# The output projection's weights and its first row tile are loaded during attention, and that tile is worked on in halves

## The reference

```python
o = bidirectional_retention(...)                      # 4 heads of 128
ret_out = silu(rg) * groupnorm(o) * ret_gn_w          # columns 0:512
mla_out = rms_norm(mla_attention(...), mla_out_norm_w)  # 8 heads of 64, columns 512:1024
mix = concatenate([ret_out, mla_out], axis=-1) @ w_out
x = layer_norm(DN_ALPHA * x + mix, ln1_w, ln1_b)
affinity = softmax(x @ w_router)                      # then: each of 16 experts picks its top tokens
```

## Time and profile before

| what | value |
|---|---|
| median of 3 runs | 3680.98 us (3678.96 to 3681.22) |
| profiled execution | 3676.88 us, its span 3675.1 us |
| TensorE busy | 3467.4 us, 94% of the span |
| DVE, ACT, POOL busy | 61%, 43%, 23% |
| attention's last DVE instruction starts | 1753.48 us |
| output stage's first DMA issue | 1757.43 us |
| first projecting matmul of tile 0, of tile 1 | 1770.85, 1791.43 us |
| output stage's last DVE instruction starts | 2105.14 us |

### The profile page before, as it was taken

The page is one execution under the profiler, slowest core; times in us unless marked ns, Lnnn a source line. Parts: engine busy times, 40 slices in busy tenths (PEclk is TensorE's granted clock), DMA queues, the critical chain, the costliest instruction groups (busy, mean ns, idle before and its releaser), DMA issues. The chain is left out here.

```text
span 3675.1 us, 51638 instructions
## 1 busy us (share of the span) xinstructions
PE 3467.4 (94%) x19042; PEld 2957.8 (80%) x19042; DVE 2239.5 (61%) x3925; ACT 1590.4 (43%) x2038; POOL 831.6 (23%) x412
## 2 busy tenths in 40 slices
PE   8999979997999999999799859999999999999996
PEld 6888868885777777777577649999999999999996
DVE  5444457776888888886455465555555555555568
ACT  2111134443676777767332223333333333333466
POOL 0000000003676767767011101111111111111101
PEclk9999989997999999999899869999999999999998
DMA  3111145656133332210433335555555555555676
GB/s 119 62 63 62 64 163 196 214 197 184 32 56 58 57 57 40 50 32 7 158 131 133 116 99 167 167 166 165 167 164 166 167 165 166 165 167 163 194 256 211
DMA packets 342352, 474.65 MB, mean 129 GB/s; under 512 B 105648, under 2 KB 241584, under 8 KB 339536
## 3 DMA queue, kind: packets, MB, share of 16 engines
q1 hardware_dynamic: 329344, 427.10, 37.1%
q0 software_dynamic: 12880, 45.88, 5.6%
HBM read 355.54 MB, written 117.39 MB: 129 GB/s over the span
## 5 line engine op out<-in xcount | busy, mean ns | idle before, releaser
L63 PE MATMUL psum<-xeT_hi,w_hi 128*128 128x320 f32 x2048 | 634.4, 310 | 0.0
L65 PE MATMUL psum<-xeT_hi,w_lo 128*128 128x320 f32 x2048 | 632.8, 309 | 0.0
L64 PE MATMUL psum<-xeT_lo,w_hi 128*128 128x320 f32 x2048 | 632.8, 309 | 0.0
L1357 POOL TENSOR_TENSOR added<-added,p_hi 128x1024 f32<-128x1024 f32 x192 | 458.8, 2389 | 157.4 <-ACT p_hi L1311 156.5
L2267 DVE TENSOR_TENSOR w_lo<-w_raw,w_hi 128x2048 fp32r<-128x2048 f32 x190 | 427.5, 2284 | 30.7 <-ACT w_hi L2102 30.7
L2102 ACT ACTIVATE w_hi<-w_raw 128x2048 fp32r<-128x2048 f32 x192 | 358.4, 1908 | 187.1 <-PE psum L65 187.1
L1393 DVE TENSOR_TENSOR p_lo<-psum,p_hi 128x1024 fp32r<-128x1024 f32 x272 | 332.5, 1222 | 89.4 <-ACT psum L1313 88.4
L63 PEld LDWEIGHTS psum<-xeT_hi,w_hi 128*128 128x128 f32 x2048 | 384.4, 188 | 0.9
L64 PEld LDWEIGHTS psum<-xeT_lo,w_hi 128*128 128x128 f32 x2048 | 384.4, 188 | 0.6
L65 PEld LDWEIGHTS psum<-xeT_hi,w_lo 128*128 128x128 f32 x2048 | 384.4, 188 | 0.0
L1311 ACT ACTIVATE p_hi<-psum 128x1024 fp32r<-128x1024 f32 x272 | 279.3, 1027 | 218.4 <-PE psum L65 218.3
(11 more groups left out here) (364 smaller groups left out, 7165.5 us busy)
## 6 DMA issues: line engine op xcount, KB each, us to landing
w_raw<-in_w_gate SPq DMA_DIRECT2D x64, 1024.0 KB, 5.2
w_raw<-in_w_up SPq DMA_DIRECT2D x64, 1024.0 KB, 7.4
w_raw<-in_w_down SPq DMA_DIRECT2D x64, 1024.0 KB, 5.4
rec<-rec SPq DMA_DIRECT2D x20, 768.0 KB, 3.6
recb<-rec SPq DMA_DIRECT2D x20, 768.0 KB, 5.0
xa<-in_x SPq DMA_DIRECT2D x20, 512.0 KB, 4.5
xb<-in_x SPq DMA_DIRECT2D x20, 512.0 KB, 5.8
v_lo_hi<-v SPq DMA_DIRECT2D x16, 640.0 KB, 9.6
```

What stands on the lines that cost most here:

```text
L63: pe.matmul(out, a[0], b[0], start=first, stop=False)
L64: pe.matmul(out, a[0], b[1], start=False, stop=False)
L65: return pe.matmul(out, a[1], b[0], start=False, stop=last)
L1357: g.tensor_tensor(acc[:], so_far, p_hi[at % 4][:].bitcast(F32), ALU.add).then_inc(s["p_added"], 1)
```

## The change

A buffer `c.shared`, 128 x (9 x 1024 + 8) float32, is allocated once for all stages. It takes the place of buffers that each stage had for itself: the weight staging, row tiles and some temporaries of the two retention stages, and the MoE stage's `w_raw` (4 x 2048) and `y_part`. Attention has nothing of its own in it; to make room there, its `added`, the first two of four `p_hi` and the first two of four `p_lo` move to memory of the latents, which attention did not use before. During attention SP loads into `shared` all 8 slices of `w_out` (two in each of the heads 1 to 4, at slots 22 and 24) and, at slot 20 of the last head, `feature_w` and tile 0 of `cat`, its attention half behind a wait for the stores of that half. The output stage then splits the slices from `shared`. Its tile 0 is turned, weighed and split in halves of 4 slices, the second half's work stands between the weight slices 0 and 1, tile 1's rms and scaling stand ahead of slice 4, and tile 1's turn behind the matmuls of slice 4. DVE's wait for the constants moves to the first use of `ln_w`.

```diff
@@ attention_phase
+        AHEAD_LOADS = {SLOTS * (n // 2 + 1) + 22 + 2 * (n % 2): n for n in range(DK)}
+        FIRST_CAT = SLOTS * (MH - 1) + 20
+        turn_at = [g + 2 for g in last_of]
-        added = [sb(f"added{b}", [P, 2, 512]) for b in range(2)]
+        wide = lambda at: at.rearrange("p (z n) -> p z n", z=2)
+        added = [wide(latents[4][:, D * b:D * (b + 1)]) for b in range(2)]
-        p_hi = [sb(f"p_hi{b}", [P, 2, 512], F32R) for b in range(4)]
-        p_lo = [sb(f"p_lo{b}", [P, 2, 512], F32R) for b in range(4)]
+        p_hi, p_lo = ([wide(latents[2 + a][:, D * b:D * (b + 1)]) for b in range(2)]
+                      + [sb(f"p_{n}{b}", [P, 2, 512], F32R)[:] for b in (2, 3)] for a, n in enumerate(("hi", "lo")))
@@ sync
+                    if g in AHEAD_LOADS:
+                        k = AHEAD_LOADS[g]
+                        sp.dma_start(wo_raw(c, k), d["w_out"][k * P:(k + 1) * P, :]).then_inc(ahead_in, 16)
+                    if g == FIRST_CAT:
+                        sp.dma_start(feature_weights(c), d["feature_w"]).then_inc(ahead_in, 16)
+                        sp.dma_start(first_cat(c)[:, 0:RW], d["ret"][0]).then_inc(ahead_in, 16)
+                        for b in range(2):
+                            sp.wait_ge(o_out[b], 16 * sum(1 for n in range(NBH) if n % 2 == b and turn_at[n] + 1 <= g))
+                        sp.dma_start(first_cat(c)[:, RW:D], d["o"][0].rearrange("p h e -> p (h e)")
+                                     ).then_inc(ahead_in, 16)
+                sp.wait_ge(ahead_in, 16 * (DK + 3))
@@ output_phase, sync
-                load_cat(0, 0)
-                sp.dma_start(fw[:], d["feature_w"]).then_inc(s["fw_in"], 16)
-                load_w(sp)
@@ tensor
+                def turn_first():
+                    for half, done in ((0, "turned_a"), (1, "turned")):
+                        if half == 1:
+                            pe.wait_ge(s["scaled"], 1)
+                        for k in range(4):
+                            at = 4 * half + k
+                            ins = pe.transpose(ps[:, half, k * P:(k + 1) * P], cat[0][:, at * P:(at + 1) * P], c.ident)
+                        ins.then_inc(s[done], 1)
                 def project_first():
-                    pe.wait_ge(s["lo_made"], 1)
+                    pe.wait_ge(s["lo_a_made"], 1)
                     for k in range(DK):
-                        pe.wait_ge(w_ready, k + 1)
+                        if k == 4:
+                            pe.wait_ge(s["lo_made"], 1)
+                        pe.wait_ge(s["w_lo_made"], k + 1)
...
-                    turn(1, 1)
+                        if k == 4:
+                            turn(1, 1)
-                turn(0, 0)
+                turn_first()
@@ scalar
-                scale(0, 0, 32)
-                make_hi(0, 0)
-                w_make_hi(a)
+                def w_make_hi(k):
+                    a.activation(w_hi[:, k, :], wo_raw(c, k), ACT.Copy).then_inc(s["w_hi_made"], 1)
+                scale(0, 0, 0)
+                a.wait_ge(s["weighted_a"], 1)
+                a.activation(cat_hi[0][:, 0:4, :], weighted[:, 0:4, :], ACT.Copy).then_inc(s["hi_a_made"], 1)
+                w_make_hi(0)
+                a.wait_ge(s["weighted"], 1)
+                a.activation(cat_hi[0][:, 4:DK, :], weighted[:, 4:DK, :], ACT.Copy).then_inc(s["hi_made"], 1)
+                for k in range(1, DK):
+                    if k == 4:
+                        scale(1, 1, 32)
+                    w_make_hi(k)
@@ vector
+                        if isinstance(u, int) and u == 1:
+                            v.wait_ge(s["const_in"], 48)
                         v.tensor_tensor(r[:], r[:], ln_w[:], ALU.mult).then_inc(s["ln_weighted"], 1)
-                v.wait_ge(s["fw_in"], 16)
+                def weigh_first(half, turned, weighted_done, hi_done, lo_done):
...
                 rms(0)
-                weigh(0, 0)
-                w_make_lo(v)
-                v.wait_ge(s["const_in"], 48)
+                weigh_first(0, s["turned_a"], s["weighted_a"], s["hi_a_made"], s["lo_a_made"])
+                w_make_lo(0)
+                weigh_first(1, s["turned"], s["weighted"], s["hi_made"], s["lo_made"])
+                for k in range(1, DK):
+                    if k == 4:
+                        rms(1)
+                    w_make_lo(k)
@@ moe_phase
-        raw = [sb(f"w_raw{r}", [P, CH]) for r in range(4)]
+        raw = [c.shared[:, CH * r:CH * (r + 1)] for r in range(4)]
-        y_part = sb("y_part", [CAP_S, 2, 512])
+        y_part = c.shared[0:CAP_S, 8 * D:9 * D].rearrange("p (a n) -> p a n", a=2)
```

More of the change, by code:

```diff
@@ L70, in bc, with wo_raw, first_cat, feature_weights @@
     return ap.unsqueeze(axis).to_broadcast(shape)
+def wo_raw(c, k):
+    return c.shared[:, D * k:D * (k + 1)]
+def first_cat(c):
+    return c.shared[:, DK * D:DK * D + D]
+def feature_weights(c):
+    return c.shared[:, 9 * D:9 * D + DK]
 class Core:
@@ L105, in split_weights @@
 def split_weights(c, ph, name, src, hi, lo, width, n_stage=2):
-    stage = [ph.enter_context(c.nc.sbuf_tensor(f"{name}_stage{b}", [P, width], F32)) for b in range(n_stage)]
+    stage = [c.shared[:, width * b:width * (b + 1)] for b in range(n_stage)]
     loaded = [c.sem(f"{name}_loaded{b}") for b in range(n_stage)]
@@ L115, in load @@
             wait_from_one(sp, lo_made, k - n_stage + 1)
-            sp.dma_start(stage[k % n_stage][:], rows[k]).then_inc(loaded[k % n_stage], 16)
+            sp.dma_start(stage[k % n_stage], rows[k]).then_inc(loaded[k % n_stage], 16)
     def make_hi(a):
@@ L1310, in exponentials @@
                     wait_p_free(a, g)
-                    a.activation(p_hi[g % 4][:], src, ACT.Exp, scale=MSCALE).then_inc(s["hi_made"], 1)
+                    a.activation(p_hi[g % 4], src, ACT.Exp, scale=MSCALE).then_inc(s["hi_made"], 1)
                     a.wait_ge(s["hi_made"], g + 1)
@@ L1429, in output_phase @@
         w_hi, w_lo = sb("wo_hi", [P, DK, D], F32R), sb("wo_lo", [P, DK, D], F32R)
-        load_w, w_make_hi, w_make_lo, w_ready = split_weights(c, ph, "wo", d["w_out"], w_hi, w_lo, D, 6)
         router = sb("router", [P, DK, E])
-        ln_w, ln_b, fw = sb("ln1_w", [P, D]), sb("ln1_b", [P, D]), sb("feature_w", [P, DK])
-        cat = [sb(f"cat{b}", [P, D]) for b in range(2)]
+        ln_w, ln_b, fw = sb("ln1_w", [P, D]), sb("ln1_b", [P, D]), feature_weights(c)
+        cat = [first_cat(c), sb("cat1", [P, D])]
         x = [sb(f"xo{b}", [P, D]) for b in range(2)]
@@ L1590, in slot @@
                                      ).then_inc(s["x1T_copied"], 1)
-                    if there(u, 1):
-                        scale(u + 1, 1 - b, u * 16 + (32 if b == 0 else 48))
+                    if there(u, 1) and not is_first(u):
+                        scale(u + 1, 1 - b, u * 16 + (32 if b == 0 else 16))
                     if there(u, -1):
@@ L2266, in chunk_lo @@
                     v.wait_ge(s["hi_made"], e * CHUNKS + (n + 1))
-                    v.tensor_tensor(w_lo[n % 4][:], raw[n % 4][:], w_hi[n % 4][:].bitcast(F32), ALU.subtract
+                    v.tensor_tensor(w_lo[n % 4][:], raw[n % 4], w_hi[n % 4][:].bitcast(F32), ALU.subtract
                                     ).then_inc(s["lo_made"], 1)
```

62 lines of the change are left out of this document (40 added, 22 removed).

## The result

| | before | after |
|---|---|---|
| median of 5 runs | 3680.98 us (3678.96 to 3681.57) | 3660.80 us (3659.98 to 3661.46) |
| profiled execution, its span | 3676.88, 3675.1 | 3660.79, 3659.0 |

The ratio is 0.9947, 95% interval 0.9932 to 0.9961.

A forecast was written before the change was run, and what follows sets the result against it. TensorE, busy 94% of the span, was taken as the bound. Tile 1's earlier start 10.1 plus clock 2.7 minus overlap 0.5 gave 12.3 us, so 3680.98 became 3668.7 us; range 3664 to 3677.

The forecast's parts named there:

- part 7: Attention: early loads and moved buffers cost 0, at most 5.2 us if exposed; tiles added to shared elsewhere also cost 0.
- rows 2 and 3: Output stage's opening (T) to tile 1's first matmul, then to tile 2's: gains forecast as 10.1 and 2.7 us.
- Parts 1 and 2: Output stage's start: loads gone, tile 0 in halves; ACT squares at opening T, first matmul at T+6.2, 7.2 us earlier.
- Part 3: Tile 0's second half between slices 0 and 1: k=1 comes 3.5 us after k=0, TensorE idles 0.9 us.
- Part 4: Tile 1's rms and scale ahead of slice 4: 2.5 us wait on DVE, up to 1.7 us of TensorE idle.
- Part 5: Tile 1's turn behind slice 4: its first matmul at T+23.9 against T+34.0, 10.1 us earlier.
- the deduction of 0.5: Taken off the sum, in us, as half of the overlap between DVE's and TensorE's bounds at tile 1's start.
- Part 6: Tile 1's clock stays high after an idle of 1.4 to 1.7 us: 2.7 us more, ends 0 and 2.7.
- A: Rival: the clock falls again ahead of tile 1, gain 9.4 to 10.1 us, 3671.2 us; chance 0.30.
- B: Rival: TensorE stays at 1.2 GHz through all of tile 0, gain 2.7 us, 3678.3 us; chance 0.06.
- C: Rival: later tiles give back at most 6 to 8 us, 3675 to 3677 us; chance 0.10.
- D: Rival: slower, attention pays for its new memory; 3695.9 us at 0.1 us a slot; chance 0.08.

The follow-up runs named there:

- e3: The kernel after with 32 unused bytes ahead of cat1, putting feature_w's bytes back at nearly their old place: 3666.75 us, ratio 0.9963.
- e11: The kernel before with 224 unused bytes ahead of the output stage's cat tiles, operand distance 0 modulo 256: 3674.73 us, ratio 0.9991.
- e7: The kernel after with tile 1's scaling and turn moved behind all eight weight slices: 3665.03 us, ratio 0.996.
- e6: The kernel after with nothing loaded during attention; tile 0, feature_w and the eight slices load at the stage's opening: 3670.26 us, ratio 0.9969.
- e12: The kernel after with 224 unused bytes ahead of the first stage's x_hi, operand distance 0 modulo 256 there: 3656.33 us, ratio 0.9934.

## Why the prediction was wrong in size, by its own steps

The step that failed is the last sentence of part 7, "The added tiles in `shared` elsewhere keep shape and engine: 0". It priced the move of buffers by what each instruction does, and left out that taking one out of a stage shifts the rest of the stage. The sum lacks a term of 4.1 us, the pace of tiles 2 to 19, and with it forecast and kernel differ by 3.8 us instead of 7.9; 3664.6 us is inside the range. What the runs showed in place of the 0: the 32 bytes of `feature_w`, moved out from between the two operands, shorten the projection's step from 233.2 to 228.1 ns; e3 gives the bytes back and loses the 4.05 us, e11 gains 4.3 without the change. The evidence was in the traces of before: matmuls 128x512 of the same three lines took 396 ns and stood 233 apart in the projection, and took 389 and stood 228 apart in the MoE stage (second line of the group of before above). The prediction took 0.232 us as the price of a matmul and did not ask why other places had less.

**The rest of the miss is mainly the reference point.** Of the 3.8 us, 1.2 are the schedule (rows 2 and 3 gave 13.5 for 12.3), 0.8 an earlier opening and 4.1 the distance from the profiled execution to the median, less 2.3 that the last stretch took longer. The forecast took the saving from the profiled execution and put it on the median, 4.1 us above that. The kernel before varied between 3674.3 and 3685.2 us in its runs here, the kernel after between 3659.98 and 3661.46. Two places of the trace vary. The stretch behind the projection's last matmul, nearly all of it the MoE stage, was 1.5 to 2.5 us shorter in the first profile than in all other traces (1587.95 against 1589.5 to 1590.5). And attention's end, from its last score to its last DVE instruction, took 14.8, 15.4, 13.7, 15.6 and 12.3 us in the five traces of placements of before, and 12.1, 15.4, 12.2, 16.0, 12.3, 12.1, 14.8, 14.8 and 12.3 in the nine of after. TensorE's row there, against the earlier trace rows (1.11 us):

```profile
1744.59 0.67 PE L1305 MATMUL psum<-p_lo,v_lo_hi 128*65 128x512 f32 x2 [2.20 <-ACT o_a L1356]
```

After the same 2.20 us of idle the clock stayed at 1.00 in the one and fell to 0.50 in the other. Both kernels show both, so it isn't the change's; whether it falls more seldom with the change, as 4 in 9 against 4 in 5 over 13 us would suggest, these traces don't settle.

The parts in turn:

- **Parts 1 and 2** held: square at T, first matmul at T+6.08 for 6.2.
- **Part 3**: k=1 came 3.38 us after k=0, forecast 3.5, with 0.48 us of idle for 0.9: six matmuls covered 2.9 us, not 2.6, since the last one counts with its whole 0.63 us and not with a step of 0.43. The part set k=1's 3.5 us against 1.2 before, the pace of the low parts; on TensorE it was 2.69 before (1770.85 to 1773.54), so the split cost TensorE 0.7 us, not 2.3.
- **Part 4**: from the end of the low part of slice 3 to the start of that of slice 4 it took 2.24 us for 2.5 (1.75 of them in front of the latter, the rest mean square and reciprocal), since from the low part's end to the scaled tile it took 1.24 us, not 1.4. TensorE idled 0.68 us, within the forecast's 0 to 1.7.
- **Part 5**: T+23.35 for T+23.9. DVE's and TensorE's bounds met, as forecast: tile 0's last matmul ended at 1778.50 and DVE began the residual at 1778.61, straight behind the low part. So the deduction of 0.5 was not needed. e7 shows that without the early turn 4.3 us of the gain are lost.
- **Part 6** held: clock 1.00 after 1.48 us of idle, gain 1.6 to 3.0 for 2.7, 0.2 of it the new pace. Tile 1 of before varied between 15.26 and 16.64 us in four traces, so the forecast, made from one, was at its upper side.
- **Part 7**: for attention the 0 held within about 1 us. From its first to its last score it took 853.2 us in the profile of after, 853.2 too in e6, which loads nothing ahead, and 852.0 to 852.8 in the traces of before: the loads cost nothing, the moved buffers at most 1.2 us over 272 slots. The other seven traces with them have 852.4 to 853.3, but for e3's 854.6. The 0 for buffers elsewhere is the step that failed.

Of the rivals, A fell with the clock at tile 1, B with the rise at 1767.9, 5.2 us after the first matmul in spite of the gap. The rule behind B (the Trainium skill, "TensorE: Matmul & The Clock Gate", section "HAM oscillation — how this bites in real kernels") describes waits longer than the work between them; here the trace has 2.9 us of work and 0.48 of wait, so its case didn't arise. C and D have nothing in the trace for them: 97.76 us of 100 busy in attention against 97.77.

## What to carry to other kernels

Moving a buffer out of a stage moves every operand behind it: compare the start-to-start step of the same matmul between places of a trace, and where it is not the same, try the distance between stationary and moving operand before crediting the edit one made. It is a thing to try and not a rule, as the second stage shows. A chain that stands ahead of a stage is worth shortening together with what queues behind its loads, for here two parts that alone gave 5.1 and 4.4 us up to tile 2 gave 13.5 together. And take a saving from several profiled executions of the kernel before, where one was 4 us below the median.

## What the runs showed of the hardware

The step between dependent-free matmuls of 128x512 with a weight load under each was 233.1 to 233.2 ns at a distance of 32 bytes modulo 256 between the operands, 233.3 at 64, 232.5 and 233.0 at 128 and 227.3 to 228.3 at 0, at a granted clock of 1.00, in two stages of the kernel. The place of either operand by itself made no difference: by the addresses in the programs both stood 224 bytes past a multiple of 256 in e11, 128 past in the first stage of e12, and at a multiple in the projection after. With DVE, ACT and POOL idle the steps of the projection were 233.3 and 226.9 ns. The Trainium skill, "TensorE: Matmul & The Clock Gate", section "Step-by-step: what each phase is for", says that TensorE reads its streamed operand and the weights through two independent ports, so that loading the next weights takes nothing from the running matmul. The traces show that some 5 ns in 233, or 2%, depend on how the two lie to each other. Whether weight load and streaming get in each other's way for them is not shown; no run here took the weight loads away. Distances other than these four weren't tried. In the second stage distance 0 came with 230.6 and 232.8 ns, and in attention, where the rows of the operands have other widths, steps of 227 to 234 ns stand side by side and weren't looked into.
